# Two-layer hybrid backbone: the products of probabilities and values, issued per group of queries in one run at one unit

## What is computed

```python
def attend(q_nope, q_rope, k_nope, k_rope, v):
    s = jnp.einsum('bqhd,bkhd->bhqk', q_nope, k_nope, preferred_element_type=jnp.float32)
    s = s + jnp.einsum('bqhr,bkr->bhqk', q_rope, k_rope, preferred_element_type=jnp.float32)
    p = jax.nn.softmax(s * ATTN_SCALE, axis=-1).astype(v.dtype)
    return jnp.einsum('bhqk,bkhd->bqhd', p, v)
```

## Time and profile before

| | |
|---|---|
| median of 3 runs | 2178.02 us (2177.92 to 2184.81) |
| span of the profiled execution (first to last instruction) | 2177.0 us |
| TensorE busy, share of the span | 2133.5 us, 98% |
| VectorE, ScalarE, GpSimd busy | 1225.2, 505.5, 900.5 us |
| DMA | 267.80 MB, mean 123 GB/s |
| attention in the trace, layer 0 and layer 1 | 421 to 584 us and 1587 to 1706 us |
| products of probabilities and values (L1063) | 416 instructions, 54.6 us busy |
| transposes (L1099) | 416 instructions, 60.6 us busy |

### The profile page before, as it was taken

One profiled execution on the slowest core, in us unless ns is written; L12 is line 12 of the kernel. 1 busy time (PEld: TensorE's weight loads), 2 busy tenths in 40 slices (PEclk: granted clock), 3 DMA queues, 4 the chain that ended last, 5 costly groups with the idle time before them and its releaser, 6 DMA issues.

```text
span 2177.0 us, 30591 instructions
## 1 busy us (share of the span) xinstructions
PE 2133.5 (98%) x12532; PEld 1774.8 (82%) x12532; DVE 1225.2 (56%) x1819; ACT 505.5 (23%) x814; POOL 900.5 (41%) x492
## 2 busy tenths in 40 slices
PE   6999999999999999999999999999999999999998
PEld 4888888877788888888888888888777787888886
DVE  7998991455663546454565424594266757253353
ACT  3115121354300220110201102322265212010010
POOL 2431443200243354444444443545411446766662
PEclk9999999999999999999999999999999999999999
DMA  7263354233553332122223254536310552322221
GB/s 281 95 143 101 114 191 140 92 119 119 199 188 126 145 122 88 58 78 87 78 88 102 78 218 186 116 138 211 119 48 23 193 184 87 107 97 97 97 97 68
DMA packets 105390, 267.80 MB, mean 123 GB/s; under 512 B 22650, under 2 KB 42490, under 8 KB 103470
## 3 DMA queue, kind: packets, MB, share of 16 engines
q1 hardware_dynamic: 68928, 190.87, 25.2%
q10 hardware_dynamic: 36334, 75.07, 10.5%
HBM read 227.56 MB, written 37.88 MB: 122 GB/s over the span
## 4 chain that ended last, share of the span: by engine, by line
PE 89%; DVE 7%; DMA 1%; ACT 1%; issue 1%; SPq 0%; POOL 0%; DVEq 0%; POOLq 0%; ACTq 0%
PE ps L469 67%; PE ps L1049 3%; PE ps L923 3%; PE ps L1063 2%; PE ps L478 2%; PE ps L1099 2%; PE ps L587 2%; DVE t_out L2218 2%; DVE t_in L2218 1%; PE ps L484 1%; PE ps L782 1%; PE ps L949 1%; PE ps L961 1%; PE ps L996 1%; PE ps L912 1%
## 5 line engine op out<-in xcount | busy, mean ns | idle before, releaser
L1291 POOL TENSOR_SCALAR whi<-raw 128x1024 fp32r<-128x1024 f32 x244 | 271.9, 1114 | 1224.0 <-PE ps L469 675.6
L1294 POOL TENSOR_TENSOR wlo<-raw,whi 128x1024 fp32r<-128x1024 f32 x244 | 629.1, 2578 | 20.4
L469 PE MATMUL ps<-hh,whi 128*128 128x512 f32 (+1 forms) x1560 | 465.3, 355 | 0.3 <-DVE ada L613 0.3
L469 PE MATMUL ps<-hh,wlo 128*128 128x512 f32 (+1 forms) x1560 | 462.6, 353 | 0.0
L469 PE MATMUL ps<-hl,whi 128*128 128x512 f32 (+1 forms) x1560 | 461.8, 352 | 0.0
L469 PEld LDWEIGHTS ps<-hh,whi 128*128 128x128 f32 x1560 | 254.7, 188 | 44.0 <-ACT mr L1724 1.0
L469 PEld LDWEIGHTS ps<-hl,whi 128*128 128x128 f32 x1560 | 254.4, 188 | 42.6 <-issue 0.2
L469 PEld LDWEIGHTS ps<-hh,wlo 128*128 128x128 f32 x1560 | 254.2, 188 | 42.2
L2151 DVE SCALAR_TENSOR_TENSOR x<-ps,ada,x 128x512 f32<-128x512 f32 x120 | 75.5, 659 | 344.8 <-PE ps L469 344.7
L469 PE MATMUL ps<-midh,whi 128*128 128x512 f32 (+1 forms) x768 | 233.7, 358 | 1.8 <-DVE midl L2181 1.8
L469 PE MATMUL ps<-midh,wlo 128*128 128x512 f32 (+1 forms) x768 | 231.2, 355 | 0.0
(11 more groups left out here) (259 smaller groups left out, 2928.7 us busy)
## 6 DMA issues: line engine op xcount, KB each, us to landing
raw<-in_w_main SPq DMA_DIRECT2D x244, 512.0 KB, 3.3
ada_gap<-in_ada_w SPq DMA_DIRECT2D x40, 512.0 KB, 10.3
ada_mixer<-in_ada_w SPq DMA_DIRECT2D x32, 512.0 KB, 4.0
g_d<-gt ACTq DMA_DIRECT2D x24, 384.0 KB, 2.4
gl<-g_d ACTq DMA_DIRECT2D x8, 1152.0 KB, 5.3
ada_first<-in_ada_w SPq DMA_DIRECT2D x16, 512.0 KB, 15.3
cout_d<-cz SPq DMA_DIRECT2D x12, 512.0 KB, 5.0
cout<-cout_d ACTq DMA_DIRECT2D x6, 1024.0 KB, 9.1
```

What stands on the lines that cost most here:

```text
L469: ins = pe.matmul(ps[:, p % 4, a:b], ww[:, w % W_SLOTS, kw * P:(kw + 1) * P], xx[:, kx, a:b], start=(first and i == 0 and j == 0), stop=(l ...
L1291: pool.tensor_scalar(whi[:, u, :], raw[:, u % 2, :], 1.0, 0.0, ALU.mult, ALU.add).then_inc(w_split.sem, 1)
L1294: pool.tensor_tensor(wlo[:, u, :], raw[:, u % 2, :], whi[:, u, :].bitcast(F32), ALU.subtract).then_inc(w_split.sem, 1)
```

## The change

The thirds of a group no longer stand at three units (5, 6, 7 for the first group, 9, 10, 11 for the second), but all three at the middle one of them (6, 10). The condition `u >= 6 and (u - 6) % 4 == 0` holds for units 6 and 10 of layer 0 and for unit 6 of layer 1. The products, their operands and their order among themselves are the same, and what is computed behind the loop is untouched.

```diff
@@ -1083,8 +1083,9 @@
                 for u, (j, b) in enumerate(units):
                     if u + 2 < len(units):
                         scores(u + 2)
-                    if u >= 5 and (u - 5) % 4 < 3:
-                        mix((u - 5) // 4, (u - 5) % 4)
+                    if u >= 6 and (u - 6) % 4 == 0:
+                        for third in range(3):
+                            mix((u - 6) // 4, third)
                     if h2 < 3 and u >= len(units) - 2:
```

## The result

The median of 20 runs of the changed kernel is 2187.26 us, against 2178.23 us for 20 runs of the kernel before: 9.0 us more. The comparable runs of both give a ratio of 1.0033, 95% interval 1.0025 to 1.0042, so slower by 7.2 us (5.4 to 9.1). The forecast was 2183.0 us in a range of 2176.0 to 2187.0: 2178.0 times the ratio is 2185.2, within it; the plain median is 0.3 us above its upper end. The direction was right. The prediction gave a change of less than 0.3% a chance of 0.79 and a slowdown beyond 0.3% one of 0.18; the measured 0.33% lies just beyond that border, and its interval (0.25% to 0.42%) on both sides of it. Against the narrower forecast of +2.8 to +7 us it is 0.2 above the upper end.

What follows compares the result with a forecast made beforehand. TensorE was taken to bound the kernel, in a loop with VectorE and ScalarE that value products cover. Layer 0's +4.6 and layer 1's +0.4 us gave +5.0, 2178.0 to 2183.0 us, range 2176.0 to 2187.0.

Steps and rivals of the forecast that it cites:

- narrower forecast: Whole program: slower by +2.8 to +7 us, the prediction's main case, given a chance of 0.66.
- T5 to T6, the long run between: Layer 0, transposes of unit 5 to those of unit 6: 3.37 us with one short run becomes 5.09.
- T6 to T7, the copy of unit 6: Layer 0, transposes of unit 6 to those of unit 7: the latter wait for ScalarE's copy to pt, 1.77 us.
- T7 to T9, VectorE's order: Layer 0, transposes of unit 7 to those of unit 9: unit 9's scaling stands behind unit 10's maximum, 3.40 us.
- T9 to the long run, the transfer: Layer 0, behind unit 9's transposes: the second modulation step waits for its DMA, so the next run starts +0.45 us late.
- last pair, T10 to T11, the copy: Layer 0's last pair, transposes of unit 10 to those of unit 11: no projection between, unit 10's copy sets 0.90 us.
- layer 1, last pair, T6 to T7: Layer 1's last pair, transposes of unit 6 to those of unit 7: only a run stood between (1.83 us); now 1.77.
- What bounds it, and that nothing covers a delay: Whole kernel: TensorE has 89% of the chain, so its delay in attention reaches the end nearly in full.
- The loop: Attention: scores, maximum, exponential, scaling, transposes, copy across TensorE, VectorE, ScalarE; value products fill its waits; layer 0 idle grows some 7 us.
- The transfer of the modulation step as the second bound at unit 9: Layer 0, unit 9: the second modulation step's DMA moves with unit 7's transposes, not unit 9's; 0.55 us per pair.
- The boundaries: Rival: 12 merged groups save up to 0.51 us each at run boundaries, -6.1 us, 2171.9; chance 0.06.
- The late transfer: Rival: the modulation transfer lands later in layer 0, 0.5 to 0.8 us more per pair, 2185 to 2187; chance 0.14.

Runs made afterwards that it cites:

- plain delay: Kernel before, with unit 11's transposes written seven times over in each pair of layer 0 and no new wait: ratio 1.0026, +5.7 us.
- late step: Changed kernel with the second modulation step of unit 9 moved to unit 11 in layer 0: ratio 1.0025, layer 0's attention 165.7 us.
- the first group alone: Kernel before with only layer 0's first group merged into one run at unit 6: ratio 1.0008, layer 0's attention 164.6 us.
- two-and-one cut with the copy covered: Kernel before with groups cut in two runs, and unit 9's second modulation step at unit 11 in layer 0's last pair: ratio 0.9995.

## Why the prediction was right, step by step

The distances between starts in the second pair of layer 0, as forecast and as they stand in the rows above:

| step | forecast | measured |
|---|---|---|
| T5 to T6, the long run between | 5.09 | 489.70 - 484.61 = 5.09 |
| T6 to T7, the copy of unit 6 | 1.77 | 491.56 - 489.70 = 1.86 |
| T7 to T9, VectorE's order | 3.40 | 494.93 - 491.56 = 3.37 |
| T9 to the long run, the transfer | 2.04 | 496.88 - 494.93 = 1.95 |
| long run to T10 | 3.88 | 500.79 - 496.88 = 3.91 |
| T10 to T11 | 1.27 | 502.07 - 500.79 = 1.28 |
| last pair, T10 to T11, the copy | 0.90 | 586.06 - 585.07 = 0.99 |
| layer 1, last pair, T6 to T7 | 1.77 | 1712.52 - 1710.67 = 1.85 |
| layer 0, all pairs | +4.6 | +4.9 |
| layer 1, all pairs | +0.4 | +0.5 |

- *What bounds it, and that nothing covers a delay:* right. The plain delay shows it by itself, 5.4 us in and 5.7 (3.1 to 8.1) out.
- *The loop:* right at each of the four waits, in place, releaser and size. TensorE's idle time in layer 0's attention was to grow by some 7 us and grew by 6.5. The one systematic miss is the handover from the end of the copy to TensorE's next start: I took a few hundredths, and it is 0.08 to 0.09 more each of nine times (T7 of all eight pairs and one T11), 0.8 us in all. That the sum came out so close is in part luck: in the second pair the transfer came 4.75 us after T7 instead of 4.87 and gave 0.1 back. From T4 to T11 the three pairs grew by 1.08, 0.96 and 0.97 (forecast 0.96) and the last by 1.84 (forecast 1.69).
- *The transfer of the modulation step as the second bound at unit 9:* right, shown by the kernel in which T9 came earlier and the time did not. Its worth was put at 0.55 us a pair. The late step gave 1.7 us in four pairs, but it paid for the moved step. The rows give the price more directly: from T9 to the run there are 493.01 - 491.64 = 1.37 us with both steps and no wait (the first group alone) and 1.95 in the changed kernel, 0.58 apart.
- *The boundaries (rival, at most 0.51 a group):* they exist. A run of 24 still takes 2.74 us, and the two-and-one cut with the copy covered turns some of them into a gain of up to 1.9 us. Their sum was put too high: the forecast wanted products cheaper by 3 to 6 us, and TensorE's busy time in the two attentions fell by 1.6 and 1.2 (118.02 to 116.79 us in layer 1's), 2.8 together. That they would decide was wrong: the waits that merging opens are larger. The Trainium skill ("TensorEngine Tiling (Array Packing)", "Tiling Modes") says that a change of tiling mode drains TensorE. Fewer changes do save time here, 3.06 - 2.74 = 0.32 us where three runs become one; that this time is the drain, and not another cost of starting a run, no run here separates.
- *The late transfer (rival, 2185 to 2187):* the total came out there, but not by this. The wait of the weight loads behind T9 grew from about 0.4 to 0.85 us, as the forecast's own term has it, and no more. A total of 2185.2 instead of 2183.0 is no support for this rival.
- *The size of the total:* the forecast of +5.0 stands against 7.2 (5.4 to 9.1). Its attention terms measure 5.4, and the plain delay shows that such a loss comes out at the end. The remaining 1 to 2 us, if they are no chance, are outside of the stages that I had costed; I had given the rest of the program nothing, and their cause is open. So the forecast is right in its mechanism, and its total lies low by what it did not cost.

## What to carry to other kernels

In a stage where TensorE is nearly always busy and still part of a loop through other engines, independent matmuls are not only work, they are the cover of the loop's waits, each at its own unit. Gather them, and the waits of the emptied units open, while the filled unit has more cover than it can use. Ask for each emptied place which wait ends there next, in order (here the copy, VectorE's order, a transfer that counts from an earlier step, and then the next copy), because removing one of two bounds in line gives next to nothing. Where an effect of a few us drowns in the program's scatter, the distance between two landmarks of the profile still tells it to about 0.3 us.

## What was not expected of the hardware

- The granted clock falls in single norm stretches in some executions: 0.63 over 6 us in one profile, 0.67 over 10 us in another, 1.00 at both places in the profile of before. TensorE is not idle there (10.00 of 10.00 us busy in the second), but at products of two columns and modulation steps. From the first of the norm's sums to the first large product behind it one such fall costs 2.4 us (12.5 instead of 10.1, the latter with 0.8 of waiting for VectorE in it) or 3.3 us (1322.9 - 1310.4 = 12.5 instead of 1316.8 - 1307.6 = 9.2), about half of the change's whole effect. It belongs to no single kernel: 11 of the 14 profiles have a fall between the two attentions, nearly all of them at one of these two norms.
- Twelve more transposes of 128x128 per pair cost 1.35 us (5.4 in four pairs), 0.11 each, in a place where I had put 0.10.
